# Attention logits of a sparse-attention layer: sign and scale moved from the exponential to the query split

## What is computed

```
score = sum over index heads of wi * relu(qi . ki), -inf above the diagonal
idx   = top_k(score, 256)                       # per query
att   = (q . k[idx]) * HEAD_DIM ** -0.5         # HEAD_DIM 64, so 1/8
att   = -inf where idx > t
out   = softmax(att) @ v[idx]
```

## Time and profile before

| | |
|---|---|
| median of 3 runs | 2279.61 us |
| lowest and highest | 2275.73 and 2281.21 us |
| profiled execution, its own time | 2281.78 us |
| its span in the trace | 2280.1 us |
| mean granted TensorE clock in it | 0.978 |
| TensorE busy | 2172.0 us (95%) |
| VectorE busy | 1302.5 us (57%) |
| ScalarE busy | 848.1 us (37%) |
| GpSimd busy | 1184.6 us (52%) |

### The profile page before, as it was taken

One profiled execution on the slowest core, in us unless ns is written; L12 is line 12 of the kernel. 1 busy time (PEld: TensorE's weight loads), 2 busy tenths in 40 slices (PEclk: granted clock), 3 DMA queues, 4 the chain that ended last, 5 costly groups with the idle time before them and its releaser, 6 DMA issues.

```text
span 2280.1 us, 31411 instructions
## 1 busy us (share of the span) xinstructions
PE 2172.0 (95%) x10040; PEld 1807.4 (79%) x10040; DVE 1302.5 (57%) x2168; ACT 848.1 (37%) x1290; POOL 1184.6 (52%) x701
## 2 busy tenths in 40 slices
PE   3879878999999999999999999999999999999999
PEld 3768667888888788888888888888888887888887
DVE  6478885498888843637777724438777543111111
ACT  4545544333233265333233243633323343332321
POOL 4678630365465400456565465646556564655653
PEclk8989978999999999999999999999999999999999
DMA  5112110232332210223333323233233333323322
GB/s 185 56 56 74 38 63 12 74 111 93 98 100 93 79 41 15 85 93 94 101 102 93 102 93 93 83 102 102 93 100 95 93 93 130 101 93 99 95 93 93
DMA packets 58546, 199.94 MB, mean 88 GB/s; under 512 B 6704, under 2 KB 6960, under 8 KB 58416
## 3 DMA queue, kind: packets, MB, share of 16 engines
q1 hardware_dynamic: 58416, 198.21, 27.7%
HBM read 193.99 MB, written 4.19 MB: 87 GB/s over the span
## 4 chain that ended last, share of the span: by engine, by line
PE 83%; DVE 6%; POOL 4%; issue 3%; ACT 2%; DMA 0%; DVEq 0%; ACTq 0%; POOLq 0%; SPq 0%
PE psum L457 26%; PE psum L458 26%; PE psum L459 25%; PE psum L624 2%; PE psum L483 2%; DVE score L1421 1%; POOL w_buf L741 1%; PE psum L601 1%; DVE s_buf L1523 1%; PE psum L540 1%; PE psum L602 1%; POOL hid_buf L741 1%; DVE small L1416 1%; DVE sq_sum L1305 1%; DVE h_buf L1297 0%
## 5 line engine op out<-in xcount | busy, mean ns | idle before, releaser
L741 POOL TENSOR_TENSOR w_buf<-raw,w_buf 128x1024 fp32r<-128x1024 f32 x336 | 815.5, 2428 | 660.4 <-ACT w_buf L947 659.7
L947 ACT ACTIVATE w_buf<-raw 128x1024 fp32r<-128x1024 f32 x336 | 353.3, 1053 | 495.9 <-PE psum L459 487.5
L457 PE MATMUL psum<-hid_buf,w_buf 128*128 128x512 f32 x1344 | 527.4, 392 | 4.6 <-DVE hid_buf L1492 2.8
L458 PE MATMUL psum<-hid_buf,w_buf 128*128 128x512 f32 x1344 | 525.0, 391 | 0.0
L459 PE MATMUL psum<-hid_buf,w_buf 128*128 128x512 f32 x1344 | 524.9, 391 | 0.0
L457 PE MATMUL psum<-h_buf,w_buf 128*128 128x512 f32 x1216 | 475.3, 391 | 1.4 <-POOL h_buf L879 1.4
L459 PE MATMUL psum<-h_buf,w_buf 128*128 128x512 f32 x1216 | 473.3, 389 | 0.0
L458 PE MATMUL psum<-h_buf,w_buf 128*128 128x512 f32 x1216 | 473.2, 389 | 0.0
L1567 DVE TENSOR_TENSOR xt<-xt,psum 128x512 f32 (+1 forms) x160 | 110.0, 688 | 359.8 <-PE psum L459 359.4
L1588 DVE SCALAR_TENSOR_TENSOR psum<-y_buf,wdw,psum 128x512 f32<-128x512 f32 x464 | 314.0, 748 | 0.0
L457 PEld LDWEIGHTS psum<-hid_buf,w_buf 128*128 128x128 f32 x1344 | 253.4, 189 | 59.0 <-DVE hid_buf L1492 3.3
(11 more groups left out here) (198 smaller groups left out, 2210.6 us busy)
## 6 DMA issues: line engine op xcount, KB each, us to landing
raw<-weights SPq DMA_DIRECT2D x352, 512.0 KB, 3.5
xt<-x_t SPq DMA_DIRECT2D x2, 2048.0 KB, 7.9
x_in<-x_t SPq DMA_DIRECT2D x12, 256.0 KB, 4.8
out_t<-xt SPq DMA_DIRECT2D x1, 2048.0 KB, 10.4
out_t<-xt SPq DMA_DIRECT2D x8, 256.0 KB, 2.0
b_tok<-x_t SPq DMA_DIRECT2D x4, 256.0 KB, 5.6
ws<-w_s SPq DMA_DIRECT2D x1, 512.0 KB, 4.1
gvb<-g_vb SPq DMA_DIRECT2D x1, 256.0 KB, 3.5
```

The source lines that it names most:

```text
L457: nc.tensor.matmul(acc, lhs_hi, rhs_hi, start=first, stop=False)
L458: nc.tensor.matmul(acc, lhs_hi, rhs_lo, start=False, stop=False)
L741: nc.gpsimd.tensor_tensor(dst_lo, raw[:, raw_slot], dst_hi.bitcast(F32), ALU.subtract).then_inc(lo_up, 1)
L947: nc.scalar.activation(dst, raw[:, raw_slot], ACT.Copy).then_inc(hi_up, 1)
```

## The change

The query split multiplies by -1/8, so both parts of the queries, and with them the logits in PSUM, come out negated and scaled. The masks change sign (+1e30), the reductions take the minimum instead of the maximum and write straight into `neg_max`, and the exponential takes scale -1 with that minimum as its bias. L1529 and the wait in front of it go, and ScalarE waits for `qk_masked`. A second triangle `tri_up` is made once, ahead of head 0, from `tri`, and TensorE waits for it at head 0. In tiles 0 and 1 VectorE now also waits for the exponential of head a - 2 before it overwrites `neg_max`.

```diff
@@ scores, TensorE
                     if t < 2:
-
-                        mm = nc.tensor.matmul(dst[:, t * P:(t + 1) * P], ident[:], tri[:], start=False, stop=True)
+                        if a == 0:
+                            pe.wait_ge(tri_made, 1)
+                        mm = nc.tensor.matmul(dst[:, t * P:(t + 1) * P], ident[:], tri_up[:], start=False, stop=True)
@@ attention, ScalarE
-                        act.wait_ge(neg_up, a + 1)
+                        act.wait_ge(qk_masked, a + 1)
...
-                                             bias=neg_max[:, a % 2:a % 2 + 1], scale=HD ** -0.5,
+                                             bias=neg_max[:, a % 2:a % 2 + 1], scale=-1.0,
@@ split_queries, VectorE
-                link(V.tensor_copy(q_stack[:, :, 0, :], q_tok[:, t]))
-                V.tensor_tensor(q_stack[:, :, 1, :], q_tok[:, t], q_stack[:, :, 0, :].bitcast(F32), ALU.subtract
-                                ).then_inc(q_split, 1)
+                link(V.tensor_scalar(q_stack[:, :, 0, :], q_tok[:, t], -(HD ** -0.5), None, ALU.mult))
+                V.scalar_tensor_tensor(out=q_stack[:, :, 1, :], in0=q_tok[:, t], scalar=-(HD ** -0.5),
+                                       in1=q_stack[:, :, 0, :].bitcast(F32), op0=ALU.mult, op1=ALU.subtract
+                                       ).then_inc(q_split, 1)
@@ mask and attention, VectorE
-                        link(V.tensor_scalar(score[t][:], score[t][:], 0.9 * TAKEN, NEG, ALU.is_gt, ALU.mult))
+                        link(V.tensor_scalar(score[t][:], score[t][:], 0.9 * TAKEN, -NEG, ALU.is_gt, ALU.mult))
...
+                if half == 0:
+                    V.tensor_scalar(tri_up[:], tri[:], -1.0, None, ALU.mult).then_inc(tri_made, 1)
...
-                    if t >= 2:
+                    logits = psum[:, 2 * (a % 2):2 * (a % 2) + 2, :].rearrange("p b n -> p (b n)")
+                    s, m = s_buf[:, a % 2], neg_max[:, a % 2:a % 2 + 1]
+                    if a >= 2:
                         dve.wait_ge(exp_up, a - 1)
...
-                                               scalar=NEG, op0=ALU.add, op1=ALU.max, accum_out=m
+                                               scalar=-NEG, op0=ALU.add, op1=ALU.min, accum_out=m
                                                ).then_inc(qk_masked, 1)
                     else:
-                        V.tensor_reduce(m, logits[:, 0:n], AX_X, ALU.max).then_inc(qk_masked, 1)
-                    dve.wait_ge(qk_masked, a + 1)
-                    V.tensor_scalar(neg_max[:, a % 2:a % 2 + 1], m, -(HD ** -0.5), None, ALU.mult
-                                    ).then_inc(neg_up, 1)
+                        V.tensor_reduce(m, logits[:, 0:n], AX_X, ALU.min).then_inc(qk_masked, 1)
```

More of the change, by code:

```diff
@@ L254, in build @@
         conv_bc, a = put("conv_bc", a, [P, HALF])
+        tri_up, _ = put("tri_up", again, [P, P])
         at_t_ring = a
@@ L281, in build @@
         neg_max = small[:, 60:62]
-        row_max = small[:, 62:64]
         r_inv = small[:, 64:72]
@@ L331, in build @@
         qk_masked = sem("qk_masked")
-        neg_up = sem("neg_up")
+        tri_made = sem("tri_made")
         exp_up = sem("exp_up")
@@ L1517, in attention @@
                     dve.wait_ge(qk_up, a + 1)
-                    if t >= 2:
+                    logits = psum[:, 2 * (a % 2):2 * (a % 2) + 2, :].rearrange("p b n -> p (b n)")
+                    s, m = s_buf[:, a % 2], neg_max[:, a % 2:a % 2 + 1]
+                    if a >= 2:
                         dve.wait_ge(exp_up, a - 1)
-                    logits = psum[:, 2 * (a % 2):2 * (a % 2) + 2, :].rearrange("p b n -> p (b n)")
-                    s, m = s_buf[:, a % 2], row_max[:, a % 2:a % 2 + 1]
                     if t >= 2:
                         V.tensor_tensor_reduce(out=s[:, 0:n], in0=logits[:, 0:n], in1=score[t][:], scale=1.0,
-                                               scalar=NEG, op0=ALU.add, op1=ALU.max, accum_out=m
+                                               scalar=-NEG, op0=ALU.add, op1=ALU.min, accum_out=m
                                                ).then_inc(qk_masked, 1)
                     else:
-                        V.tensor_reduce(m, logits[:, 0:n], AX_X, ALU.max).then_inc(qk_masked, 1)
-                    dve.wait_ge(qk_masked, a + 1)
-                    V.tensor_scalar(neg_max[:, a % 2:a % 2 + 1], m, -(HD ** -0.5), None, ALU.mult
-                                    ).then_inc(neg_up, 1)
+                        V.tensor_reduce(m, logits[:, 0:n], AX_X, ALU.min).then_inc(qk_masked, 1)
                     if h == 2 and t % 4:
```

## The result

| | before | after |
|---|---|---|
| median of 5 runs each | 2278.94 us | 2267.26 us |
| lowest and highest | 2275.73, 2281.21 | 2265.26, 2269.72 |
| ratio, 95% interval | | 0.995, 0.9936 to 0.9965 |
| profiled execution, its own time | 2281.78 | 2267.50 |
| its span | 2280.1 | 2265.8 |

Two repeats gave ratios of 0.9958 (0.9945 to 0.9971) and 0.9951 (0.9938 to 0.9965), gains of 9.8 and 12.8 us by the medians.

A forecast was written before the change was run, and what follows sets the result against it. VectorE was taken to bound heads 0 to 23, TensorE heads 24 to 31 and the second half. First half 4.5 us plus second half 1.8 made 6.3 us, a median of 2273.3 us, range 2268.5 to 2278.0.

The forecast's parts named there:

- The worth of one in tiles 0 and 1: VectorE's queue, tiles 0 and 1: each removed L1529 gives back 0.24 us, 0.12 for its slot and 0.12 for its wait.
- the empty pipe: Rival, tiles 0 and 1: next operation waits for an empty pipe, 0.16 us a head, 5.3 us in all; chance 0.08.
- The exponential 0.04 us behind its releaser: ScalarE: released by the accumulator read, the exponential starts 0.04 us behind it, 0.18 us earlier than before.
- The split at its old price: Query split: its copy becomes a multiplication at 0.43 us, its difference a fused one at the old time; cost taken as 0.
- no effect: Rival: the minimum form holds the exponential or next search as long as L1529 did; 2279.6 us, chance 0.05.
- a slower kernel: Rival, tile 3: the clock drop lasts longer, up to 17.3 us lost and 2290.6 us; chance 0.02.
- TensorE takes over sooner: Rival, tiles 1 and 2: TensorE's lag stays small, only heads 0 to 6 and second half count; 3.5 us, chance 0.12.
- I take 0.13 us a head: Tile 2: search can't start before about 0.08 to 0.12 us after the accumulator read; 8 x 0.13 = 1.0 us.
- the new wait for TensorE: Heads 7 to 11: VectorE would wait for head 12's logits, so five removed instructions give 0.4 us, not 1.2.
- the cover of heads 24 to 63: Tile 3 and second half: only places with visible TensorE waits gain, 0.36 and 1.8 us; remaining heads give nothing.
- three places: Tile 5: TensorE waits of 0.25, 1.50 and 0.40 us lose 0.18, 0.11 and 0.18, together 0.47 us.
- The clock stays up: Rival, tile 3: the clock drop may not come, 3.3 us more, 9.6 in all, 2270.0 us; chance 0.15.

The follow-up runs named there:

- The pair with fillers: Kernel before and changed kernel, each with small unused matmuls in TensorE's stalls: 2274.47 and 2265.57 us, ratios 0.9985 and 0.9949 to before.
- the second trace of the kernel before: The kernel before, unchanged, run and traced again: ratio 0.9997 (0.9988 to 1.0006).
- its repeat: The changed kernel, unchanged, run and traced again: 2268.84 against 2278.61 us, ratio 0.9958.
- the slot back: Changed kernel with the 128x1 multiplication and its wait put back into VectorE's queue, result unused: 2274.91 us, ratio 0.9983.
- The shifts: Linked memsets on VectorE ahead of head 0: ten or thirteen in the changed kernel (2273.39, 2275.66 us), eleven in the kernel before (2280.00 us).
- late exponential: Changed kernel with a dependent 128x1 copy on ScalarE ahead of every exponential: 2272.29 us, 3.4 above the change.
- shifted kernel before: Kernel before with eleven linked memsets on VectorE ahead of head 0, a shift of 2.44 us: 2280.00 against 2279.04 us, ratio 1.0006.
- small shift: Changed kernel with ten linked memsets on VectorE ahead of the triangle, a shift of 2.75 us: 2273.39 us, ratio 0.9979.

## Why the prediction was wrong

**The sum by stages.** The forecast comes, for tiles 0, 1, 2, 3 with the end, and the second attention, to 1.8, 1.3, 1.0, 0.4 and 1.8 us, together 6.3. The pair with fillers, whose later drops are out, gave 1.8, 1.2, 1.8, 1.3 and 2.7, together 8.8.

**Right.** The place: heads 0 to 23 are VectorE's, and an instruction less in its queue counts there. The worth of one in tiles 0 and 1: 0.24 us, from starts 0.20 and 0.33 us apart. By the rule of the empty pipe, which the section "The DRAIN you can't avoid" of the Trainium skill (VectorE: DVE Perf Modes) begins with, they would be 0.28 and 0.41 apart; neither is. What the section adds, that an operation that is not held starts earlier, fits these rows. The exponential 0.04 us behind its releaser. The split at its old price where nothing disturbs it (0.42 and 0.69), the triangle (0.22 us, in VectorE's idle time). The rivals of the empty pipe, of no effect and of a slower kernel fall, and so does "TensorE takes over sooner", since tiles 1 and 2 gave 1.2 and 1.8 us.

**Mis-sized, tile 2.** "I take 0.13 us a head": the search starts with the accumulator read, 0.00 us behind it, so a head gives 0.23 and the tile 1.81 us instead of 1.0. My lower bound of 0.08 was the length of the read. I had not applied to it what I read from the earlier trace rows, a start 0.08 us before the end of the one ahead, which gives just the 0.00 measured.

**Failed, the new wait for TensorE.** The prediction says of heads 7 to 11 that "these five give 0.4 us and not 1.2: the new wait is VectorE for the logits of head 12". There is no such wait. In the trace after TensorE finishes those logits at about 332.05 and VectorE takes them at 334.24. The 0.20 us of slack belonged to one execution with a long drop: in the second trace of the kernel before, whose drop ended earlier, TensorE was 1.78 us early at the same head. In the changed kernel it was 2.19 us early, and in the repeat 0.88. A wait of this kind did come at another head. Mask and first reduction of tile 2, in the trace after and in its repeat:

```profile
340.78 0.35 DVE L1512 TENSOR_SCALAR score<-score 128x384 f32<-128x384 f32 x1
341.55 0.56 DVE L1527 CUSTOM_DVE_ANT_0 s_buf<-psum,score 128x384 f32<-128x384 f32 x1 [0.42 <-DVE score L1512]
```

```profile
342.02 0.35 DVE L1512 TENSOR_SCALAR score<-score 128x384 f32<-128x384 f32 x1
342.49 0.56 DVE L1527 CUSTOM_DVE_ANT_0 s_buf<-psum,score 128x384 f32<-128x384 f32 x1
```

They start 0.77 and 0.47 us apart. In the first trace TensorE had been at 1.2 GHz from 336.4 to 339.8 us and its logits of head 16 end at 341.40, later than the mask; that is the 0.3 us by which tile 1 is longer there (15.99 against 15.71).

The gain over heads 7 to 11 is nevertheless small, 10.73 - 10.15 = 0.58 us, for a reason that I had priced at nothing: the split has moved under a GpSimd instruction. VectorE's and GpSimd's timeline, tile 1, after:

```profile
331.43 0.54 DVE L1440 TENSOR_SCALAR q_stack<-q_tok 128x512 fp32r<-128x512 f32 x1
...
331.63 0.91 POOL L770 TENSOR_TENSOR q_tok<-q_tok,pool_tmp 128x256 f32<-128x256 f32 x1
332.00 1.09 DVE L1441 SCALAR_TENSOR_TENSOR q_stack<-q_tok,q_stack 128x512 fp32r<-128x512 f32 x1
```

0.54 and 1.09 us where they take 0.42 and 0.69 alone: 0.52 us lost. 10.73 - 5 x 0.24 + 0.52 = 10.05, near the 10.15 seen. In the kernel before GpSimd had ended that work 0.46 us ahead of the split (333.64 and 334.10). With the slot back, which has the changed kernel's split, GpSimd ended at 334.87 and the split, from 335.5 on, took 0.43 and 0.69 us again. No run moved GpSimd's instruction alone. Tile 1 as a whole gave 0.9 to 1.2 us, near the 1.3 that my two wrong terms made.

**Failed, the cover of heads 24 to 63.** "The remaining heads give nothing; TensorE's own work covers them." Tile 3 with the end gave 1.29 us, not 0.36, and the second half 2.73, not 1.8. I counted places where the timeline shows a wait. TensorE's timeline after, tile 5, against the earlier trace rows:

```profile
810.33 0.63 PE L483 MATMUL psum<-ident,a_tok 128*128 128x128 f32 x4 [0.25 <-issue]
...
813.41 0.41 PE L483 MATMUL psum<-ident,p_buf 128*128 128x128 f32 x2 [1.32 <-DVE hid_buf L1494]
...
818.45 0.66 PE L483 MATMUL psum<-ident,q_stack 128*128 128x128 f32 x4 [0.20 <-ACT pt_buf L1065]
```

The third wait went from 0.40 to 0.20 as reckoned. The second went from 1.50 to 1.32 and not by 0.11: nothing now stands between the read and L1494, which starts 0.00 us behind it and not 0.19. The first did not shrink, and still the heads around it came 0.18 us closer. Tile 5 has four distances that shrank (behind heads 41, 43, 44 and 45), where I had counted three places. Matmul ends in a trace are modelled, so a wait of 0.2 us can hide inside a row that looks busy; that is my reading, not shown.

**Failed, the clock.** The prediction wanted "the first attention 4.5 us shorter, the second 1.8, all else equal", and priced the clock ("The clock stays up") for tile 3 alone, at 3.3 us with a chance of 0.15. With tiles and second attention corrected the sum is 8.8 us, and 8.9 was measured with the later drops out of both kernels. That alone would have given 2279.6 - 8.8 = 2270.8, inside the stated range. Outside the attention the kernel before has two drops of 1.6 us behind stalls in the second half, and the traces of the changed kernel have none: 3.2 us more. Inside it the changed kernel pays more for drops than the kernel before, 1.6 us in the second attention (a gain of 1.17 in place of 2.73) and up to 0.3 in tile 1. Together that makes 10.1 us, and by the table the second trace of the kernel before and the trace after differ by 10.2. The first trace of the kernel before had 4.2 us more, in tile 3 and the MLP, so its median should hold some of that; how much of the remaining 1.5 of the 11.7 us this is, no run shows. As for tile 3 itself, its clock did stay up, but it did in the unchanged kernel's second trace too.

The shifts show that the drops of the rest hang on where the stalls fall in time. That the time fell by 11.7 us and not by about 9 is thus no work of the change, but a position of the stalls that a shift undoes. I had written that where drops fall may differ from run to run: for tile 3, the MLP and tile 1 that is what the repeats show. The two drops of the rest and those of the second attention were the same in all traces of a kernel, and without fillers they moved with every shift. Either way they belong in the range of every small change.

**Left open.** Outside tile 2, how much of the late exponential's 3.4 us the copy costs and how much the clock. What makes the drops of tile 3 and the MLP come in one execution and not in the next. Why the shifted kernel before got its drops inside the second attention.

## What to carry to other kernels

Price a tiny instruction that waits for the one ahead of it by the distance of starts with and without it (here 0.24 us for a 128x1 multiplication of 0.15), and fold its arithmetic into something that is computed anyway. Where stalls may or may not be followed by a clock drop, compare variants stage by stage and not by the total, with more than one trace each: a shift of 2.75 us cost 5.9. Short unused matmuls in TensorE's stalls kept this kernel's rest free of drops at the one shift tried, for no measurable cost.

## What the hardware did that I had not expected

- Behind the same stall of 1.8 us the granted clock was 0.72 or 1.00 over the next 6 us. Which of the two changed with a shift of all that comes later, and was the same in all traces of a kernel (2 of 2 of the kernel before, 3 of 3 of the changed one). The Trainium skill (TensorE: Matmul & The Clock Gate, "Part 1: The HAM clock gate") says that the activity monitor runs free of the kernel, and that the point of transition varies with where the first matmul falls; the shifted runs agree, and so does the spread of single executions of the small shift, 2267.80 to 2276.27 us.
- Behind an accumulator read of 0.08 us an independent VectorE instruction started in the same 0.01 us, whatever it was: the search, the split, `cat`, the mask (all 24 in the trace after that followed within 0.7 us).
- A two-input VectorE instruction of 0.69 us took 1.09 us where it started beside a GpSimd two-input instruction, and the multiplication by a constant 0.54 instead of 0.42.
